# The first layer's feed-forward for context and latents side by side, 512 moving columns in place of twice 256

## The reference, cut to what matters

```
h  = modulate(rmsnorm(x,  norm1_g[l]), sh1,  sc1)        # latents
hc = modulate(rmsnorm(xc, norm1_g[l]), csh1, csc1)       # context
...                                                      # conv branch + attention, gated, @ w_out[l]
x  = x + g1 * gated_merge(...)
x  = x + g2 * conv_ffn(modulate(rmsnorm(x, norm2_g[l]), sh2, sc2), w_up[l], ffn_dw[l], ffn_dw_b[l], w_down[l])
if not last:                                             # layer 0 only
    xc = xc + cg1 * gated_merge(...)
    xc = xc + cg2 * conv_ffn(modulate(rmsnorm(xc, norm2_g[l]), csh2, csc2), same four arrays)

def conv_ffn(h, w_up, dw, dw_b, w_down):
    u = dwconv1d(h @ w_up, dw, dw_b)                     # 3 taps along the tokens
    a, g = jnp.split(u, 2, axis=-1)                      # 2816 + 2816 channels
    return (jax.nn.silu(g) * a) @ w_down
```

## Time and profile before

| | |
|---|---|
| median of 3 runs | 2270.96 us (2266.97 to 2273.97) |
| profiled execution, its span | 2270.7 us |
| TensorE (PE) busy | 2201.9 us, 97% |
| VectorE (DVE) busy | 1817.6 us, 80% |
| ScalarE (ACT) busy | 1297.3 us, 57% |
| DMA | 499.80 MB, mean 220 GB/s |
| chain that ended last | PE 71%, DVE 14%, ACT 6%, DMA 4%, issue 4% |

### The profile page before, as it was taken

The page is one execution under the profiler, slowest core; times in us unless marked ns, Lnnn a source line. Parts: engine busy times, 40 slices in busy tenths (PEclk is TensorE's granted clock), DMA queues, the critical chain, the costliest instruction groups (busy, mean ns, idle before and its releaser), DMA issues.

```text
span 2270.7 us, 49231 instructions
## 1 busy us (share of the span) xinstructions
PE 2201.9 (97%) x18008; PEld 2118.6 (93%) x18008; DVE 1817.6 (80%) x3186; ACT 1297.3 (57%) x2102; POOL 119.8 (5%) x231
## 2 busy tenths in 40 slices
PE   7998999999999999999999999999999999999998
PEld 5897999998899999889999999997999999989998
DVE  4886877799699978978998878877878877888655
ACT  3465765536776554576665644657544644686443
POOL 0100000000000100000000001000000001000000
PEclk8999999999999999999999999999999999999999
DMA  9846676765358875535788687673777677636654
GB/s 364 276 140 206 232 240 223 244 201 163 117 178 277 273 236 195 175 114 174 238 279 270 228 282 261 219 256 109 257 268 266 237 277 260 236 116 203 219 166 132
DMA packets 150550, 499.80 MB, mean 220 GB/s; under 512 B 17408, under 2 KB 21632, under 8 KB 148864
## 3 DMA queue, kind: packets, MB, share of 16 engines
q1 hardware_dynamic: 113504, 374.01, 48.1%
q0 software_dynamic: 32544, 119.55, 16.4%
q10 hardware_dynamic: 4352, 4.20, 0.6%
HBM read 496.65 MB, written 1.05 MB: 219 GB/s over the span
## 4 chain that ended last, share of the span: by engine, by line
PE 71%; DVE 14%; ACT 6%; DMA 4%; issue 4%; ACTq 0%; DVEq 0%; POOL 0%; POOLq 0%; SPq 0%
PE bank_pair L1971 21%; PE bank_pair L1973 21%; PE bank_pair L1972 21%; DVE w_lo L1201 4%; DMA modraw<-in_w_mod 2%; ACT w_hi L648 2%; DVE arena L1488 2%; PE bank_pair L2098 2%; PE ps_o L1984 1%; DVE arena L1357 1%; DVE small L1602 1%; ACT arena L911 1%; DVE h_lo L1366 1%; PE ps_o L2485 1%; DMA raw<-in_w_gu 1%
## 5 line engine op out<-in xcount | busy, mean ns | idle before, releaser
L1201 DVE TENSOR_TENSOR w_lo<-raw,w_hi 128x1024 fp32r<-128x1024 f32 (+2 forms) x748 | 823.0, 1117 | 189.8 <-ACT w_hi L648 186.7
L648 ACT ACTIVATE w_hi<-raw 128x1024 fp32r<-128x1024 f32 (+2 forms) x748 | 713.1, 966 | 391.0 <-PE bank_pair L1973 254.4
L1971 PE MATMUL bank_pair<-h_hi,w_hi 128*128 128x256 f32 x2928 | 837.3, 286 | 10.2 <-DVE arena L1801 4.2
L1972 PE MATMUL bank_pair<-h_lo,w_hi 128*128 128x256 f32 x2928 | 828.8, 283 | 0.0
L1973 PE MATMUL bank_pair<-h_hi,w_lo 128*128 128x256 f32 x2928 | 828.7, 283 | 0.0
L1971 PE MATMUL bank_pair<-e_both,w_hi 128*128 128x256 f32 (+1 forms) x2064 | 592.1, 287 | 8.7 <-DVE w_lo L1201 5.0
L1971 PEld LDWEIGHTS bank_pair<-h_hi,w_hi 128*128 128x128 f32 x2928 | 561.8, 192 | 27.4 <-issue 19.7
L1973 PE MATMUL bank_pair<-e_both,w_lo 128*128 128x256 f32 (+1 forms) x2064 | 584.3, 283 | 0.0
L1972 PE MATMUL bank_pair<-e_both,w_hi 128*128 128x256 f32 (+1 forms) x2064 | 584.2, 283 | 0.0
L1972 PEld LDWEIGHTS bank_pair<-h_lo,w_hi 128*128 128x128 f32 x2928 | 562.2, 192 | 0.3
L1973 PEld LDWEIGHTS bank_pair<-h_hi,w_lo 128*128 128x128 f32 x2928 | 562.1, 192 | 0.0
(11 more groups left out here) (250 smaller groups left out, 2106.4 us busy)
## 6 DMA issues: line engine op xcount, KB each, us to landing
modraw<-in_w_mod POOLq DMA_DIRECT2D x216, 512.0 KB, 5.3
raw<-in_w_gu SPq DMA_DIRECT2D x176, 512.0 KB, 4.6
raw<-in_w_up SPq DMA_DIRECT2D x132, 512.0 KB, 5.1
raw<-in_w_gate SPq DMA_DIRECT2D x48, 512.0 KB, 3.9
raw<-in_w_dn SPq DMA_DIRECT2D x64, 384.0 KB, 4.6
raw<-in_w_dn SPq DMA_DIRECT2D x64, 320.0 KB, 3.6
raw<-in_w_down SPq DMA_DIRECT2D x48, 384.0 KB, 5.1
raw<-in_w_down SPq DMA_DIRECT2D x48, 320.0 KB, 4.8
```

The costliest lines, as they stand in the source:

```text
L648: nc.scalar.activation(w_hi[:, p, HALF * f:HALF * f + w], raw[:, p, HALF * f:HALF * f + w], ACT.Copy)\
L1201: nc.vector.tensor_tensor(w_lo[:, p, at], raw[:, p, HALF * f:HALF * f + w], w_hi[:, p, at].bitcast(F32), ALU.subtract).then_inc(lo_ready, 1)
L1971: nc.tensor.matmul(out, l[0], r[0], start=start, stop=False)
L1972: nc.tensor.matmul(out, l[0], r[1], start=False, stop=False)
```

## The change

Both attention halves of layer 0 now come first, and one feed-forward follows for both streams. `ffn_joint` makes it in two parts: up slabs 0 to 11, down part 0, up slabs 12 to 21, down part 1. Each matmul moves 512 columns: in up, the latents' and the context's normed parts (`h_joint`, two rows of 256 that lie a fixed distance apart, since the context's now live in the arena as `c_hi`, `c_lo`); in down, `e_joint`, in which the two streams' columns lie side by side. Taps run over two rows of 255. The first two up slabs do the context's columns first and then the latents'; the last two down slabs likewise. The context's second norm (norm 2) is not folded: its slots lie in the latents' merge and out; the latents' first norm has its slots in the context's merge and out; the latents' second norm is fused but not folded; the context's first norm of layer 1 follows the joint down.

```diff
-N_PE = 33
+N_PE = 32
...
-    layer_a(0, "ctx")
-    layer_a(0, "x")
-    norm("ctx", "a", 1, 0, N_MOD_A + 8, dest="e")
+    norm("ctx", "a", 0, 0, 8)
+    attention(0, "ctx")
+    norm("ctx", "a", 0, 3, 20, dest="c")
+    attention(0, "x")
+    norm("x", "a", 0, 3, 20, fold=False)
+    ffn_joint()
+    norm("ctx", "a", 1, 0, N_MOD_A + 8, dest="c")
     stage("q", a["w_k1"], SLAB, 1, arg=dict(dst="kc", rope=False, scale=1.0, conv=None))
     stage("v", a["w_v1"], SLAB, 1, arg=dict(dst="vc", conv=None, heads=NA_H))
-    layer_a(1, "x")
+    norm("x", "a", 1, 0, N_MOD_A + 8)
+    attention(1, "x")
+    ffn_a(1, "x")
...
+    def ffn_joint():
+
+        part0 = None
+        for part, (j0, n) in enumerate(((0, FA), (FA, FC - FA))):
+            stage("upa", a["w_up0"], SLAB, n // 2, mods=2, arg=dict(l=0), joint=True, j0=j0)
+            stage("down", a[f"w_down0{part}"], n * P, 4, kc=n, mods=2 * int(part == 0), joint=True, part0=part0,
+                  arg=dict(x="ctx", kind="a", l=0, v=5, need=N_MOD_A, part=part))
+            part0 = plan[-1][1]
...
+            def joint_half(s, b, p, f):
+
+                pe.wait_ge(lo_ready, 2 * (s.l0 + 2 * b + p) + f + 1)
+                if s.kind == "upa":
+                    for k in range(DC):
+                        c = HALF * f + P * k
+                        x = [h_joint[:, :, (DC * e + k) * T:(DC * e + k + 1) * T] for e in range(2)]
+                        ins = mm3(both(pb[p][:, f, :]), (w_hi[:, p, c:c + P], w_lo[:, p, c:c + P]), x, k == 0, k == DC - 1)
+                else:
+                    n = s.kc // 2
+                    for k in range(n):
+                        c = HALF * f + P * k
+                        x = [e_joint_part(e, n * f + k) for e in range(2)]
+                        ins = mm3(pb[p][:, 0, :], (w_hi[:, p, c:c + P], w_lo[:, p, c:c + P]), x, k == 0 and not f,
+                                  k == n - 1 and f == 1)
+                ins.then_inc(half_done, 1)
...
+                elif ctx_first(s, b):
+
+                    if p == 0:
+                        joint_one(s, 0, 1)
+                        free_banks(s, b, 1, False)
+                        joint_one(s, 1, 1)
+                        joint_one(s, 0, 0)
+                        norm_sum(norms[s.norm_i])
+                    else:
+                        joint_one(s, 1, 0)
+                else:
+                    for f in range(2):
+                        if s.kind == "down" and is_first and p == 0:
+                            pe.wait_ge(up_lo, up_done[id(s)] + FC - (1 - f) * s.kc // 2)
+                        joint_half(s, b, p, f)
...
                 sweep(dve, s, body)
-                tail_mul(s.e0 + FC, 1)
-                tail_lo(s.e0 + FC, 1, FC - 1)
+                n = 2 * s.bodies
+                tail_mul(s.e0 + n, 1)
+                tail_lo(s.e0 + n, 1, n - 1)
...
+                if n["fused"] and n["before"].joint:
+                    joint_product(n["before"], DC - 1, 1, "x")
```

More of the change, by code:

```diff
@@ L290, in build @@
             s.fold = s.after if s.after["fold"] else None
+            if s.kind == "merge":
+                s.after = None
+            if s.kind == "glu" and waiting is not None:
+                s.after, waiting = waiting, None
         last_entry = (what, s)
@@ L521, in whole @@
         def whole(s):
-            return s.kind == "upa"
+            return s.kind == "upa" and not s.joint
         def last_turn(s, b, p):
```

363 lines of the change are left out of this document (279 added, 84 removed).

## The result

| | before | after |
|---|---|---|
| median of the runs, same chip | 2272.47 us (2266.97 to 2278.97, 20 runs) | 2276.77 us (from 2274.67, 20 runs) |
| ratio to before, 95% interval | | 1.0019 (1.0012 to 1.0026) |
| span of the profiled execution | 2270.7 us | 2274.8 us |
| DMA | 499.80 MB | 465.12 MB |
| granted TensorE clock, mean of the span | 0.995 | 0.989 |

The change is 0.2% slower, 4.3 us. The forecast was 20 us faster, its range ended at 2266. The change moves 35 MB less weight data and takes 96 us of work off VectorE, and gains nothing. (One run of the changed kernel, at 4277.69 us, is a disturbed one: it counts in the median, which is 2276.57 without it, and not in the ratio.)

What follows compares the result with a forecast made beforehand. TensorE, 97% busy, was taken as the bound, its matmuls paced by weight loads; -34.3 - 1.0 + 3.0 - 9.7 + 13.8 + 5.5 + 1.5 + 1.0 = -20.2 us gave 2250.5, range 2243 to 2258, or 2236 to 2266 with three rivals.

Steps and rivals of the forecast that it cites:

- The matmuls: Both feed-forwards on TensorE: 1428 matmuls of 512 columns at 0.216 us plus 312 at 0.120, 345.9 for 380.2 us: 34.3 less.
- rival B: Joint matmuls: the weight load adds its 11 ns to any width, 227 ns each; 15.5 us more, 2266; chance 0.06.
- The estimate from the Trainium skill: Feed-forward matmuls: columns already set the pace at 256 (109 ns, weight load 107), 216 ns at 512; gain only 3.8 us.
- The context's merge: Context's merge stage: norm work moved in, its fourth slab getting eight scalings (3.25 us); 1.5 us more.
- Seams: Joint up to down, twice: TensorE idles 5.6 us on up's last low part, plus 1.3 for the clock; 13.8 more for both.
- End of the joint stage: After joint down: TensorE idles 3.1 us for the context's next norm, low parts 1.1, clock 1.3; 5.5 us more.
- Tiles in the latents' attention: Latents' glu, q, k, v and merge: moved modulation turns wait for single-buffered 1 MB tiles; 3 us more (0 to 12).
- A turn: TensorE's modulation turn: 1.1 us each, from 23.5 us for 21 turns; one turn fewer, 1.0 us less.
- Rival D: Latents' attention: single-buffered tiles starve it, eight turns at 1.3 to 1.7 us; 9 us more, 2259; chance 0.10.
- rival C: Joint up: VectorE becomes the bound, 11 us a slab for 10.4; 12 us more, 2262; chance 0.12.
- the weights: Feed-forward weights: 38 slabs loaded and split once instead of twice, 34.6 MB less on SP's queue; costed at nothing.

## Why the prediction was wrong

**The matmuls: the step that failed.** "So at full clock the pace is the weight load's, and 13 ns of every matmul are columns not sent." With 512 columns they do not go away: an addition of 13 ns comes at full clock with every width from 256 on, and at 512 it is the same with 32, 64 or 128 columns of weights. Only at 256 was the weight load part of it, 6 or 7 of the 13 ns. 1428 matmuls at 0.2267 in place of 0.216 are 15.3 us, so the matmuls went from 380.2 to 361.2: 19.0 less, not 34.3. This is rival B's number, 227 ns and 15.5 us, given a chance of 0.06, though B's mechanism is not borne out: fewer columns of weights do not lower the 227. It was dismissed by the earlier trace rows: no addition at half clock was taken as no addition at all. The changed kernel shows 426.7 at half and 226.7 at full clock for one form, so that inference does not hold: something that is 13 ns at one level is absent at the other. And the value of the earlier trace rows was carried from plain fp32 over to one-pass fp32, which is another kind of matmul. The estimate from the Trainium skill ("TensorE: Matmul & The Clock Gate", Back-to-back issue gap) was weighed wrongly too: that columns more than weights set the pace at 256 was nearer to what was measured, 113 ns being left there with narrow weights. Its gain of 3.8 us, from some 109 and 216 ns, is too small, since 120 and 227 were measured.

**The context's merge: 1.5 forecast, 6.6 measured.** The step counted the norm moved there and not the silu of the vector, which the diff moves there as well. The cost of a moved step includes its table loads: 1.91 us became 4.5. With the norm's sum (3.3) the stage is 5 us over the forecast, though the 4.0 us of tile waits that it had before are gone.

**Seams: right in mechanism, near in size.** 5.1 and 5.8 us of waits, on the operation named, against 5.6 forecast; the last low part's matmul came 9.57 us behind up's last one, forecast 9.7. The clock behind them cost more: ten and eight matmuls and a slower one at either end, 2.6 and 2.1 us counted from the distances, against 1.3 each. Counted from start to start the two seams cost 15.8 us (5.26 and 5.93 above the usual 0.227, and the clock's 4.6) where 13.8 were forecast. That two modulation products stand in that chain was in the forecast; that they could be taken out and half a slab put in was not asked.

**End of the joint stage.** 3.2 for the context's norm, as forecast (3.1). A wait was overlooked behind it: the latents' norm of layer 1 can begin only after the same down stage, and its sum costs 3.0 in the context's k stage.

**Tiles in the latents' attention.** 2.1 us of waits for a tile in v and 2.4 for turns' columns stand against 3. In their merge, and ahead of their first out slab,

```profile
PE bank_pair L2178 <- DVE w_lo L1312: 4.7, 2, 3.3
```

for low weight parts stand against 1.0 (before there were 1.4). In all the latents' attention and merge are 7 us longer beyond the 13 of the ten turns, where 4 were forecast. A turn was put at 1.1 us, from the busy time of its records, and costs 1.3 from start to start. Rival D did not come.

**VectorE (rival C) and the weights.** 82% and 77% busy against 85 to 90 forecast, no regular wait for low weight parts. Of the 96 us taken off VectorE, 93 off ScalarE and 35 MB of loads nothing shows in the time, as the forecast had it.

**The sum, with what was measured**: -19.0 for -34.3 (15.3), context's merge 5.1 more, latents' attention and merge 3, seams 2.0, the start 1.2 (not shown to be the change's), and some 2 the other way from the rest bring -20.2 to +4. With the first term alone put right the forecast would have been 4.9 us faster, less than the 6.8 that it called measurable; it took the context's merge and the small terms to make the change slower.

## What to carry to other kernels

Before an addition to an instruction's pace is called another resource's, test it on a second size of the same form and type, at the same clock: two widths tell a floor from an addition, one width at two clocks does not. When one stage is cut into parts so that a consumer follows its producer sooner, look at how many instructions stand between them on every engine, and give the consumer the half that doesn't need the last result; here the half alone was worth 12.5 us by the spans, where the change lacked 4 to break even. An instruction moved across a change of function table costs its loads too, and it costs the same again wherever its engine is next on the path.

## What the hardware did that was not expected

- One-pass fp32 matmuls of 256 to 512 columns start columns/2.4 GHz + some 13 ns apart (20 ns at 448), bf16 ones columns + 2.5. At the lower clock one-pass fp32 has no addition: 213.3 and 426.7 ns.
- The weight load's floor for this type is 111 ns with 128 moving columns; with 32 or 64 columns of weights such matmuls start about 60 apart, and matmuls of 256 columns then start 113 or 114 apart in place of 120.
- Idle time alone does not tell whether the clock falls: a wait of 3.0 us ahead of joint down (with VectorE's products behind the low part) left it up, one of 2.15 in the earlier trace rows did not. One and the same wait, 3.3 us ahead of the latents' first out slab, left it up in the changed kernel's trace, and the granted clock fell around it in the trace with the silu in the joint up stage (at 434.49) and in that with the silu in ScalarE's gap (at 436.37).
